# Gate and up columns of a feed-forward block as seven block products in place of eight

## The reference

```python
h2 = rms_norm(x, norm_ffn[l])
x = x + (jax.nn.silu(h2 @ w_ffn_gate[l]) * (h2 @ w_ffn_up[l])) @ w_ffn_down[l]
...
x = x + 0.5 * swiglu(rmsnorm(x, ffn1_norm[l]), ffn1_w1[l], ffn1_w3[l], ffn1_w2[l])
...
x = x + 0.5 * swiglu(rmsnorm(x, ffn2_norm[l]), ffn2_w1[l], ffn2_w3[l], ffn2_w2[l])
```

## Time and profile before

| | us |
|---|---|
| median of three runs (3230.3 to 3232.1) | 3230.31 |
| span of the profiled execution | 3228.2 |
| outside the span (median less span) | 2.1 |
| PE, matmuls busy | 3208.3 |
| PEld, weight loads busy | 2632.0 |
| DVE busy | 1695.3 |
| ACT busy | 1164.5 |

### The profile page before, as it was taken

How to read it: one execution, slowest core, us unless ns; L and a number is a source line. 1 busy time by engine, 2 the same in 40 slices (tenths; PEclk the granted TensorE clock), 3 DMA queues, 4 the chain that set the end, 5 groups by cost and what they waited for, 6 DMA issues and landing times.

```text
span 3228.2 us, 39623 instructions
## 1 busy us (share of the span) xinstructions
PE 3208.3 (99%) x14786; PEld 2632.0 (82%) x14786; DVE 1695.3 (53%) x2482; ACT 1164.5 (36%) x1847; POOL 0.2 (0%) x4
## 2 busy tenths in 40 slices
PE   9999999999999999999999999999999999999999
PEld 7777778788888888888887888888888888788887
DVE  6564455564544545346755554344543676465443
ACT  5673555532222222233533322222222344332222
POOL 0000000000000000000000000000000000000000
PEclk9999999999999999999999999999999999999999
DMA  4333333232222222232322222222223233132222
GB/s 146 102 95 98 97 100 105 85 117 93 97 98 98 96 94 96 98 114 79 118 85 66 94 95 97 98 98 94 95 98 103 97 98 111 46 105 97 93 96 92
DMA packets 90696, 313.32 MB, mean 97 GB/s; under 512 B 10192, under 2 KB 12624, under 8 KB 90192
## 3 DMA queue, kind: packets, MB, share of 16 engines
q1 hardware_dynamic: 83376, 294.69, 27.5%
q10 hardware_dynamic: 7200, 16.97, 1.7%
HBM read 309.52 MB, written 2.10 MB: 97 GB/s over the span
## 4 chain that ended last, share of the span: by engine, by line
PE 95%; DVE 2%; ACT 2%; issue 1%; DMA 0%; SPq 0%; ACTq 0%; DVEq 0%
PE ps L1101 29%; PE ps L1103 29%; PE ps L1102 29%; PE ps L1300 1%; PE ps L1386 1%; PE ps L1289 1%; PE ps L1177 1%; PE ps L1399 0%; PE ps L1423 0%; PE ps L1334 0%; PE ps L1281 0%; PE ps L1338 0%; PE ps L1278 0%; PE ps L1317 0%; PE ps L1328 0%
## 5 line engine op out<-in xcount | busy, mean ns | idle before, releaser
L1101 PE MATMUL ps<-x_hi,whi 128*128 128x512 f32 x2400 | 945.0, 394 | 0.0
L1103 PE MATMUL ps<-x_hi,wlo 128*128 128x512 f32 x2400 | 934.6, 389 | 0.0
L1102 PE MATMUL ps<-x_lo,whi 128*128 128x512 f32 x2400 | 934.0, 389 | 0.0
L1440 ACT ACTIVATE whi<-raw 128x1024 fp32r<-128x1024 f32 (+1 forms) x555 | 583.1, 1053 | 895.3 <-DMA raw<-in_weights 893.2
L1727 DVE TENSOR_TENSOR wlo<-raw,whi 128x1024 fp32r<-128x1024 f32 x553 | 675.3, 1223 | 418.5 <-ACT whi L1440 409.7
L1101 PEld LDWEIGHTS ps<-x_hi,whi 128*128 128x128 f32 x2400 | 450.7, 188 | 97.2 <-issue 3.9
L1103 PEld LDWEIGHTS ps<-x_hi,wlo 128*128 128x128 f32 x2400 | 450.5, 188 | 94.6
L1102 PEld LDWEIGHTS ps<-x_lo,whi 128*128 128x128 f32 x2400 | 450.8, 188 | 94.2 <-issue 2.4
L1101 PE MATMUL ps<-h_hi,whi 128*128 128x512 f32 (+1 forms) x902 | 346.4, 384 | 0.0
L1103 PE MATMUL ps<-h_hi,wlo 128*128 128x512 f32 (+1 forms) x902 | 346.2, 384 | 0.0
L1102 PE MATMUL ps<-h_lo,whi 128*128 128x512 f32 (+1 forms) x902 | 346.2, 384 | 0.0
(11 more groups left out here) (295 smaller groups left out, 3303.7 us busy)
## 6 DMA issues: line engine op xcount, KB each, us to landing
raw<-in_weights SPq DMA_DIRECT2D x553, 512.0 KB, 3.3
bias<-in_biasB ACTq DMA_DIRECT2D x16, 384.0 KB, 3.2
bias<-in_biasA ACTq DMA_DIRECT2D x16, 256.0 KB, 3.2
mem_raw<-in_mem ACTq DMA_DIRECT2D x3, 1024.0 KB, 7.0
x_res<-in_x SPq DMA_DIRECT2D x8, 256.0 KB, 6.6
x_res<-in_x ACTq DMA_DIRECT2D x8, 256.0 KB, 3.2
out_x<-x_res SPq DMA_DIRECT2D x16, 128.0 KB, 1.8
raw<-in_weights SPq DMA_DIRECT2D x2, 256.0 KB, 4.0
```

The costliest lines, as they stand in the source:

```text
L1101: pe.matmul(out, hi, xhi, start=start, stop=False)
L1102: pe.matmul(out, hi, xlo, start=False, stop=False)
L1103: return pe.matmul(out, lo, xhi, start=False, stop=stop)
L1440: return act.activation(out, in_, ACT.Copy, scale=scale)
```

## The change

The first pair of inner rows (f = 0 and 1) is computed as before (`plain`, 4 units). The other 20 are taken in ten pairs. For pair i, gate and up weights of both rows form a matrix of two by two blocks, rows f=2i and 2i+1 by features 0 to 511 and 512 to 1023: A11, A12, A21, A22, each 8 tiles (4 gate, 4 up) in one 512 KB set. The activations are also two by two blocks: feature halves by token halves of 256. The Winograd form of Strassen's scheme needs seven products of blocks, P1 to P7, each 8 tiles by three matmuls of 256 columns, where the plain way needs the equivalent of eight. Four of the seven stationary operands are sums of weights, made on VectorE from the loaded blocks (`wsum`: S1 = A21+A22, S2 = S1-A11, S3 = A11-A21, S4 = A12-S2); all seven are then split into high (`whigh`, ScalarE) and low (`wlow`, VectorE). Of the moving operands four are sums (`tform`), made once per feed-forward block for each of four feature rows and split as well (`thigh`, `tlow`).

The products meet in PSUM and in SBUF: ScalarE copies the partial sums after P1, P5 and P6 out (`kept`), VectorE adds them to the others (`block`: C11, C12, C22, C21) and multiplies by the norm's factor (`rmul`). The high part of the row is now written by ScalarE (`fhigh`).

The down projection runs in blocks of four rows (two pairs): after every odd and even pair, all 8 columns take 4 tiles each (12 matmuls) and are added to the residual; the last six rows follow at the end, in two parts for columns 0 to 3 (P4 of pair 10 lies between) and in one part for columns 4 to 7. The last column, in halves of 256 tokens (`closing`), holds 6 tiles in place of 22. So a column is added to the residual five or six times.

The hardware loops are gone: every step is written out, and SyncE's loads follow the same list, among them those of the sets (`wload`), each waiting for the product that last used its buffer. Six sets of a block are loaded behind column 3 of the projection ahead of it; three of the four moving sums are made between that projection's last columns (`toward_ffn`).

Shortened to its core:

```diff
     step("reload", m=DC - 1)
     norm = 1
 
+    def toward_ffn(m, n, gain, j):
+
+        if m == 3:
+            for i, form in [(1, form) for form in SET] + [(2, "A21"), (2, "A22")]:
+                step("wload", n=n, i=i, form=form, free=("evac", j))
+        if m >= 4:
+            if m < DC - 1:
...
+                step("tlow", n=n, p=m - 5)
+
+    def moving_sums(n, p, gain):
+
+        step("xt", n=n, p=p, gain=gain)
+        step("tform", n=n, p=p)
+        step("thigh", n=n, p=p)
...
+    def ffn(w1, w3, w2, l, c, n, gain, gain_next, back=False):
+
+        u0 = len(s.units)
+        for f in range(2):
             for w in (w1, w3):
                 s.unit(w, l, [(k, f) for k in range(DC)])
-        s.open_units(t0 // UT + AHEAD - 1)
...
+        for i in range(1, PAIRS):
+            s.sets.append((n, i, w1, w3, l))
+        for b in range(4):
+            for m in range(0, DC, 2):
+                s.unit(w2, l, [(4 * b + k, m + mm) for mm in range(2) for k in range(4)])
+        order = ([(16 + k, m) for m in range(4) for k in range(4)] + [(20 + k, m) for m in range(4) for k in range(2)]
+                 + [(16 + k, m) for m in range(4, DC) for k in range(6)])
...
+        def form_step(kind):
+            return lambda i, *forms: [step(kind, n=n, i=i, form=form, behind=u0 + 3) for form in forms]
+        total, high, low = form_step("wsum"), form_step("whigh"), form_step("wlow")
...
+        s.open_units(u0 + AHEAD - 1)
+        step("ffn", n=n)
+        step("plain", n=n, unit=u0, c=0)
+        step("fsum", n=n)
+        s.open_units(u0 + 2)
+        moving_sums(n, 3, gain)
+        step("tlow", n=n, p=2)
+        total(1, "S1")
+        high(1, "S1", "A11")
+        total(1, "S3", "S2")
+        low(1, "A11")
+        high(1, "S2")
+        step("froot", n=n)
+        step("fscale", n=n, unit=u0, c=0)
+        row("silu", 0)
+        step("plain", n=n, unit=u0 + 1, c=1)
+        s.open_units(u0 + 3)
+        step("tlow", n=n, p=3)
+        low(1, "S1")
+        step("fscale", n=n, unit=u0 + 1, c=1)
+        row("fmul", 0)
+        row("fhigh", 0)
+        step("plain", n=n, unit=u0 + 2, c=2)
+        total(1, "S4")
+        low(1, "S2")
+        row("flow", 0)
+        high(1, "A12")
+        low(1, "A12")
+        step("fscale", n=n, unit=u0 + 2, c=2)
+        row("silu", 1)
+        step("plain", n=n, unit=u0 + 3, c=3)
+        step("fscale", n=n, unit=u0 + 3, c=3)
+        row("fmul", 1)
+        row("fhigh", 1)
+        high(1, "S4", "S3")
+        row("flow", 1)
+        low(1, "S4", "S3")
+
...
+        def odd_pair(i):
+
+            y, o = i + 1, i - 1
+            product(i, "P1")
+            load(y, "A11", (i, "P1"))
+            kept(i, "P1")
+            s.open_units(u0 + 4 + 4 * (i // 2) + 3)
+            if o:
+                product(o, "P4")
+                load(y, "A22", (o, "P4"))
+                block(o, "C21")
+                row("silu", 2 * o + 1)
+            high(y, "A11")
+            if o:
+                row("fmul", 2 * o + 1)
+                row("fhigh", 2 * o + 1)
+            product(i, "P5")
+            kept(i, "P5")
+            if o:
+                row("flow", 2 * o + 1)
+            high(i, "A22")
+            low(i, "A22")
+            total(y, "S1")
+            high(y, "S1")
+            product(i, "P6")
+            kept(i, "P6")
+            total(y, "S3", "S2")
+            low(y, "A11")
+            high(y, "S2")
+            product(i, "P2")
+            load(y, "A12", (i, "P2"))
+            block(i, "C11")
+            low(y, "S1")
+            product(i, "P3")
+            block(i, "C12")
+            step("rmul", n=n, i=i, row=0)
+            row("silu", 2 * i)
+            total(y, "S4")
+            high(y, "S4")
+            row("fmul", 2 * i)
+            row("fhigh", 2 * i)
+            product(i, "P7")
+            load(i + 2, "A21", (i, "P7"))
+            block(i, "C22")
+            row("flow", 2 * i)
+            step("rmul", n=n, i=i, row=1)
+            low(y, "S2")
+            high(y, "S3", "A12")
+
...
+        for b in range(4):
+            odd_pair(2 * b + 1)
+            even_pair(2 * b + 2)
+            q = 2 * b + 3
+            fs = range(4 * b, 4 * b + 4)
+            for m in range(DC):
+                if m == 0:
+                    total(q, "S4")
+                    high(q, "S4")
+                elif m == 1:
+                    low(q, "S2")
+                    high(q, "S3")
+                elif m == 2:
+                    low(q, "S4")
+                    high(q, "A12")
...
+                down((u0 + 4 + 4 * b) * UT + 4 * m, fs, m, fs if m == 0 else ())
+        odd_pair(9)
+        even_pair(10)
+        fs, t1 = range(16, NF), (u0 + 20) * UT
+        for m in range(4):
+            if m == 2:
+                product(10, "P4")
+                block(10, "C21")
+                row("silu", NF - 1)
+                row("fmul", NF - 1)
+                row("fhigh", NF - 1)
+                row("flow", NF - 1)
+            down(t1 + 4 * m, fs[0:4], m, fs[0:4] if m == 0 else ())
+        step("ffn_end", n=n)
         for m in range(DC - last):
...
+            late = m < 4
+            j = down(t1 + (16 + 2 * m if late else 6 * m), fs[4:] if late else fs, m, fs[4:] if m == 0 else (),
+                     "back" if back else "resid")
             step("refresh", n=n + 1, m=m, gain=gain_next, need=("x", m) if back else ("evac", j))
+            if back or gain_next.startswith("ffn1"):
+                toward_ffn(m, n + 1, gain_next, j)
         if last:
-            closing(t1 + (DC - 1) * NF, c, n + 1, gain_next)
+            closing(t1 + 6 * (DC - 1), c, n + 1, gain_next)
...
+                elif kind == "prod":
+                    n, i, name = a["n"], a["i"], a["name"]
+                    form = FORM_OF[name]
+                    low = FORM_LOW[place_of(i, form)]
+                    pe.wait_ge(*on("form_ready", (n, i, form)))
+                    if i == 1 and name in MOVING:
+                        pe.wait_ge(*on("tl", (n, 3)))
...
+                        pe.wait_ge(*on(*{"P6": ("kept", (n, i, "P1")), "P7": ("kept", (n, i, "P6")),
+                                         "P4": ("block", (n, i, "C22"))}[name]))
+                    opens = name in ("P1", "P2", "P5")
+                    for at in range(UT):
+                        w, k = divmod(at, 4)
+                        if name in MOVING:
+                            xhi, xlo = (t[:, k, MOVING[name], :] for t in (TH, TL))
+                        else:
+                            kk, tokens = (k + (0 if name == "P1" else 4)), slice(HALF, T) if name == "P3" else slice(0, HALF)
+                            xhi, xlo = (t[:, kk, tokens] for t in (XH, XL))
+                        to = out[:, w * HALF:(w + 1) * HALF]
+                        hi, lo = high_tile(form, at), low[:, at * P:(at + 1) * P]
+                        pe.matmul(to, hi, xhi, start=opens and at == 0, stop=False, skip_group_check=True)
+                        pe.matmul(to, hi, xlo, start=False, stop=False, skip_group_check=True)
+                        mm = pe.matmul(to, lo, xhi, start=False, stop=at == UT - 1, skip_group_check=True)
+                    mm.then_inc(*sig("prod", (n, i, name)))
...
+                    copy(high_form(form), form_in_rows(FORM[place_of(i, form)])).then_inc(*sig("form_hi", (n, i, form)))
+                elif kind == "kept":
+                    n, i, name = a["n"], a["i"], a["name"]
+                    act.wait_ge(*on("prod", (n, i, name)))
+                    if i > 1:
+                        act.wait_ge(*on("block", (n, i - 1, {"P1": "C11", "P5": "C22", "P6": "C12"}[name])))
+                    copy(kept_in(name), PS[:, 1, :] if name == "P5" else chain_bank(i)).then_inc(*sig("kept", (n, i, name)))
...
+                    dve.wait_ge(*on("form_hi", (n, i, form)))
+                    if form in ("A11", "A22", "A12", "S1", "S2"):
+                        reader = {"A11": "S2", "A22": "S1", "A12": "S4", "S1": "S2", "S2": "S4"}[form]
+                        dve.wait_ge(*on("form", (n, i, reader)))
+                    dve.tensor_tensor(form_in_rows(FORM_LOW[place]), form_in_rows(FORM[place]), high_form(form).bitcast(F32),
+                                      ALU.subtract).then_inc(*sig("form_ready", (n, i, form)))
...
+                elif kind == "block":
+                    n, i, name = a["n"], a["i"], a["name"]
+                    of, kept, by, to = {"C11": (PS[:, 2, :], "P1", "P2", 0), "C12": (PS[:, 1, :], "P6", "P3", 1),
+                                        "C22": (chain_bank(i), "P5", "P7", 2), "C21": (chain_bank(i), None, "P4", 1)}[name]
...
+                    if kept:
+                        dve.wait_ge(*on("kept", (n, i, kept)))
+                        dve.tensor_tensor(to, in_halves(of), in_halves(kept_in(kept)), ALU.add).then_inc(*sig("block", (n, i, name)))
...
```

431 lines of the change are left out of this document (308 added, 123 removed).

## The result

The change took 3280.11 us as the median of 4 runs (3278.78 to 3280.59), the kernel before 3231.14 beside it; the ratio is 1.0151 (95% interval 1.0137 to 1.0166). It is slower by 49 us; 3274 was forecast, 43.5 above the old time.

The account below looks back on a forecast made before the run. TensorE, its matmuls busy 99% of the span, was taken as the bound. Added 10 + 22 + 33 + 28 + 28 + 6 = 127 us, removed 83.5: +43.5, giving 3274 us, range 3212 to 3314.

Parts of the forecast that it names:

- The saving: Ten pairs in five blocks: 168 narrow matmuls take 20.08 us where wide ones took 21.75, saving 83.5 us in all.
- (a): Three starts behind a mixer: moving sums between late columns delay column 7's x_lo, 6.4 us once, 7.8 twice; 22 us.
- (d): First pair of each feed-forward block: late scaling and ScalarE copies keep products waiting, 5.6 us five times; 28 us.
- (b): Two starts behind a down projection: late columns too short to cover the refresh, 13.5 and 19.5 us late; 33 us.
- (c): Fourth plain unit at each start: ready after 17.9 us where TensorE needs 12.3; 5.6 us five times, 28 us.
- The clock: Behind the stops TensorE may drop to the lower clock: bounds 0 and 15 us, taken as 0.
- The steady pairs: P4 waits for C22 about 0.5 us per block of two pairs, 4 blocks, 5 times: 10 us.
- Returns and end: Feed-forward to mixer, twice, 2 us each, and the shorter last column at the kernel's end, 2: 6 us.
- 1: Rival: the waits (c) and (d) at the starts don't arise; 3218 us, faster; chance 0.12.
- 3: Rival: the clock falls after the stops, adding 15 us; 3289 us, slower; chance 0.08.
- 4: Rival: narrow products pay for new weight loads, 31.9 us a pair for 21.75, +508; 3740 us; chance 0.02.
- 5: Rival: VectorE bounds the steady pairs, 5 us lost per block of two pairs, +90; 3363 us; chance 0.05.

Follow-up runs that it names:

- run 1: The change with each pair's 168 matmuls of 256 columns replaced by 96 of 512, all waits, sums and splits kept: 3337.75 us.
- Run 5: The change with unread matmuls given to TensorE during the stops at the starts, to keep it busy: 3279.75 us.
- run 9: The change with ScalarE's copies of P5 and P6 put ahead of the high parts of the next pair's A11 and S1: 3300.21 us.
- run 2: The change with the fourth plain unit rounded and split just ahead of the norm's root, not behind the first silu: 3270.68 us.
- run 7: The change with the unit of weights put ahead of the moving sums between a projection's late columns, on ScalarE and VectorE: 3262.54 us.
- run 3: The change with P4 of the pair before put behind P5, not ahead of it, in even pairs: 3263.16 us.

## Why the prediction was right, point by point

**The saving.** 83.5 us was the number of matmuls times the two distances of the earlier trace rows. Both distances were measured again, and run 1 gives two pairs and a down part their 65.28 us back. Right.

**The starts, (a) to (d).** 22 + 33 + 28 + 28 = 111 were forecast. A start and TensorE's own 59.5 us in it can be measured directly, from the first gate matmul to the first down matmul, with the stops in the late down part ahead of it where there is one.

| start | forecast | length | above 59.5 | stops ahead | measured |
|---|---|---|---|---|---|
| n=1 | 17.6 | 696.03 to 773.01, 77.0 | 17.5 | | 17.5 |
| n=2 | 30.7 | 1064.08 to 1150.44, 86.4 | 26.9 | 4.9 | 31.8 |
| n=3 | 19.0 | 1802.03 to 1880.44, 78.4 | 18.9 | | 18.9 |
| n=4 | 24.7 | 2167.70 to 2250.77, 83.1 | 23.6 | 0.9 | 24.5 |
| n=5 | 19.0 | 2900.88 to 2977.93, 77.1 | 17.6 | | 17.6 |
| sum | 111.0 | | | | 110.3 |

The forecast of a start is its (a) or (b) with 5.6 for (c) and 5.6 for (d). Within a start the terms were less good, and as idle time alone they come to about 78 us, not 111. At n=1 the stop for `x_lo` was 5.47 (6.4 forecast), that for the fourth unit 3.52 (5.6), those of the first pairs 0.52 and 2.17 (5.6 in all). At n=2 and 4 the stops for `x_lo` came to 11.0 and 10.5 (with the stops ahead of the first gate column 15.9 and 11.4, where 19.5 and 13.5 were forecast). The copy of P1, which was to be late at every start, was so at one (1.5 us, n=2); C22 of the first pair took its place. (d) was a coarse sum over waits that mostly arose elsewhere, and that it fits the total this well is in part luck. The difference is matmuls that take longer behind a stop, at the lower clock and while they restart: TensorE is busy 65.3 us in the first start where its own work is 59.5, and 332 in all five, 35 more than five times 59.5. Run 5, where the first start runs at full clock and takes as long, shows that the slow matmuls are no term of their own.

What was right is when VectorE lets TensorE go on. The last `x_lo` was walked to 706.7 at n=1 and came at 706.54. The fourth unit was walked to 17.9 us behind it, 724.6, and came at 724.18. At n=2 and 4 the last `x_lo` was walked to 46.0 and 40.0 us behind the start of the late part (1037.32 and 2144.78), which is 1083.3 and 2184.8; TensorE went on at 1082.69 and 2184.16. The stops are shorter than forecast because TensorE, slower behind each stop, arrives later at the next. The length of a start is what VectorE's list takes with its waits for ScalarE, and it was that list I had walked.

**The clock.** "Bounds 0 and 15; I take 0, because what follows each stop is bounded by VectorE." Run 5 shows it: full clock in the first start (0.994 over the whole kernel against 0.987), same time. The granted clock did fall, just behind the 3.5 us stop (and behind the 5.5 us one, to 0.50 for 3.4 us):

```profile
724.00:730.00 6.00, 5.82 (x14) 4.62 (x15) 5.79 (x7) 1.58 (x2) 0.00 (x0) 0.51 0.01 3
```

That is what the Trainium skill ("TensorE: Matmul & The Clock Gate", section "Why this matters for your kernels") says of idle TensorE. The 15 us that the forecast would have added for it did not come, because in the starts TensorE isn't the one behind.

**The steady pairs.** 0.5 us were forecast for C22 in each block of two pairs; 0.31 and the restart are 0.47 (818.30 less the start before it, 817.71, less 0.12). A block takes 62.63 us against 2 x 20.08 + 21.75 = 61.91 of matmuls: 14.4 us in 20 blocks, 10 forecast. The other 0.25 us lie among the 336 narrow matmuls, under 0.001 each, a term I had left out.

**Returns and end.** 6 us were forecast. The stretches from a feed-forward block to the next through a mixer grew by 3.5 us each (1437.13 to 1802.03, 364.90, against 361.37 before), 7 in all. Half of it is the stop for `x_lo` behind the feed-forward block (1.56 and 1.52); the other half is a stop of 1.58 ahead of the first gate column of n=3 and 5, which belongs to the starts and is missing in the table. So the starts cost some 3 us more than forecast, and the returns some 0.5 less.

Together 110.3 + 14.4 + 7 - 83.5 = 48.2, of 49.7 us between the two spans; the 1.5 left were not followed up, and the end of the kernel, forecast at 2, lies in them. The 6 us by which the forecast was low are the steady pairs' 4.4 and part of the two stops ahead of n=3 and 5.

**The rivals.** 1 (waits (c) and (d) don't arise): they arose, at a little over half size each (16 us of 28 in both), with the rest in the slow matmuls behind each stop. The prediction named waits under half of its figures as a sign of being wrong. The stops for `x_lo` (5.4 to 5.5 behind the mixers, 11.0 and 10.5 at the other two) and for the fourth unit (2.2 to 3.5, only one of them under half of 5 to 6) mostly stay above it; the copy of P1, late once, doesn't. 3 (the clock): fell, cost nothing. 4: out by run 1; the additional weight loads bring PEld to 84%, and every steady pair runs at 0.12 us a matmul. 5: VectorE was busy 191.7 of 250 us in the steady part, 77%, and the stop stayed at 0.3; in run 9 one high part in another place made it 1.2.

## What to carry to other kernels

This block scheme saved 83.5 us of matmuls and, in every order tried, lost at least as much elsewhere: the best kernel is level with the one before. It lost most of it where its operands are first made, and little in the steady part. Add up each in-order list from the last cover to the first product, and compare it with TensorE's time over the same stretch. In such a stretch the stops, the restarts and the lower clock are one quantity, set by that list with its own waits for the next engine. Taking away the lower clock alone gave nothing (run 5), and of one stop taken away two thirds came back as the next (run 2); changing what stands ahead of a wait in the list (run 7, run 3) gave 17 us each. Before a step is put ahead on one engine, look at who waits for what is then behind it: run 9 lost 20 us by letting a copy go first that nobody in the steady pairs was waiting for.
